# Mamba core of a hybrid backbone: decays requested ahead, token-major group sums, the first two output chunks together

## What is computed

```python
# 32 heads in 8 groups of 4; head width 64, state 128, chunk of 128 tokens
cb = jnp.einsum('bclgn,bcsgn->bgcls', cc, bc)
y_diag = jnp.einsum('bgcls,bgrcls,bcsgrp->bclgrp', cb, decay_in, x)
y_off = jnp.einsum('bclgn,bcgrpn,bgrcl->bclgrp', cc, prev_states, jnp.exp(a_cs))
y = y_diag + y_off                       # forward, and flipped for backward
y = y + d_skip * xs
y = y * jax.nn.silu(z)
yg = y.reshape(b, L, SSM_GROUPS, SSM_INNER // SSM_GROUPS)
yg = yg * lax.rsqrt(jnp.mean(yg * yg, axis=-1, keepdims=True) + EPS)
h = h + mod[:, :, 5] * ((yg.reshape(b, L, SSM_INNER) * norm_w) @ out_w)
```

## Time and profile before

| | us |
|---|---|
| median of 3 runs | 2073.91 |
| lowest, highest | 2071.22, 2076.09 |
| the profiled execution | 2077.36 |
| its span in the profile | 2075.5 |
| PE busy in the span | 1993.5 (96%) |
| DVE, ACT, POOL busy | 1295.8, 677.1, 203.0 |

### The profile page before, as it was taken

The page is one execution under the profiler, slowest core; times in us unless marked ns, Lnnn a source line. Parts: engine busy times, 40 slices in busy tenths (PEclk is TensorE's granted clock), DMA queues, the critical chain, the costliest instruction groups (busy, mean ns, idle before and its releaser), DMA issues. The chain is left out here.

```text
span 2075.5 us, 24931 instructions
## 1 busy us (share of the span) xinstructions
PE 1993.5 (96%) x10168; PEld 1666.4 (80%) x10168; DVE 1295.8 (62%) x1816; ACT 677.1 (33%) x900; POOL 203.0 (10%) x140
## 2 busy tenths in 40 slices
PE   7999999999999989999999999999999988789998
PEld 4788888878888878888887888888788984489998
DVE  5655547687877675554677555476765768745544
ACT  4422222232211242222223222222443546534432
POOL 1000001100034300000110000011000004430001
PEclk9999999999999999999999999999999999899999
DMA  9544426543520244442645444265443526554554
GB/s 358 198 146 133 161 69 203 165 151 125 176 86 1 81 164 141 160 145 90 195 147 170 149 131 154 74 206 157 152 142 92 164 87 190 156 162 151 186 156 138
DMA packets 279297, 306.73 MB, mean 148 GB/s; under 512 B 9457, under 2 KB 249745, under 8 KB 277393
## 3 DMA queue, kind: packets, MB, share of 16 engines
q1 hardware_dynamic: 275392, 293.83, 44.5%
q10 hardware_dynamic: 3792, 11.34, 1.4%
HBM read 298.70 MB, written 6.43 MB: 147 GB/s over the span
## 5 line engine op out<-in xcount | busy, mean ns | idle before, releaser
L1541 PE MATMUL banks<-xh,wh 128*128 128x512 f32 (+1 forms) x2120 | 775.5, 366 | 19.8 <-DVE xl L994 13.8
L1542 PE MATMUL banks<-xl,wh 128*128 128x512 f32 (+1 forms) x2120 | 771.6, 364 | 0.0
L1543 PE MATMUL banks<-xh,wl 128*128 128x512 f32 (+1 forms) x2120 | 771.4, 364 | 0.0
L929 DVE TENSOR_TENSOR wl<-raw,wh 128x2048 fp32r<-128x2048 f32 (+1 forms) x195 | 404.1, 2072 | 277.7 <-ACT wh L575 276.7
L575 ACT ACTIVATE wh<-raw 128x2048 fp32r<-128x2048 f32 (+1 forms) x201 | 349.8, 1740 | 637.4 <-PE banks L1543 557.8
L1541 PEld LDWEIGHTS banks<-xh,wh 128*128 128x128 f32 x2120 | 403.5, 190 | 88.4 <-issue 15.4
L1543 PEld LDWEIGHTS banks<-xh,wl 128*128 128x128 f32 x2120 | 403.3, 190 | 62.5
L1542 PEld LDWEIGHTS banks<-xl,wh 128*128 128x128 f32 x2120 | 403.8, 190 | 61.4
L1541 PE MATMUL banks<-gh,wh 128*128 128x512 f32 (+1 forms) x704 | 255.7, 363 | 3.7 <-DVE wl L929 2.5
L1542 PE MATMUL banks<-gl,wh 128*128 128x512 f32 (+1 forms) x704 | 255.2, 363 | 0.0
L1543 PE MATMUL banks<-gh,wl 128*128 128x512 f32 (+1 forms) x704 | 255.2, 362 | 0.0
(11 more groups left out here) (219 smaller groups left out, 1709.9 us busy)
## 6 DMA issues: line engine op xcount, KB each, us to landing
raw<-in_ffn_in SPq DMA_DIRECT2D x88, 1024.0 KB, 5.1
raw<-in_ffn_out SPq DMA_DIRECT2D x64, 704.0 KB, 4.8
ada_rawf<-in_ada_rest SPq DMA_DIRECT2D x60, 512.0 KB, 3.4
ada_rawo<-in_ada_rest SPq DMA_DIRECT2D x48, 512.0 KB, 3.3
raw<-in_mb_in_w SPq DMA_DIRECT2D x24, 1024.0 KB, 5.4
raw<-in_hy_in_w SPq DMA_DIRECT2D x12, 1024.0 KB, 5.2
afb<-decays SPq DMA_DIRECT2D x32, 256.0 KB, 4.7
raw<-in_mb_out_w SPq DMA_DIRECT2D x8, 1024.0 KB, 5.5
```

The lines of the kernel that those rows point to most:

```text
L929: dve.tensor_tensor(wl[n_slot][:, 0:cols], raw[r_slot][:, 0:cols], wh[n_slot][:, 0:cols].bitcast(F32), ALU.subtract).then_inc(w_lo, 1)
L1541: pe.matmul(dst, h, x_hi, start=start, stop=False)
L1542: pe.matmul(dst, h, x_lo, start=False, stop=False)
L1543: return pe.matmul(dst, l_, x_hi, start=False, stop=stop)
```

## The change

- **SP** runs one loop over 34 steps: at step h it requests afb of head h (after e_done and d_done count h-3, as before), then csx of head h-2 (after cs_used, as before). So csx stands two heads behind afb in the queue.
- **x of the latent tokens**: only x = 8 and 9 are turned and scaled ahead of b_dot_c(0). PE's turn_x(10 + 2g + p) stands behind the csx matmuls of pair p in groups 0 to 2 (bank 7), DVE's token_major(10 + 2g + r//2) behind exponents in heads 1 and 3 of these groups. d_x waits for the transposes it needs.
- **square_y** writes tt2 and tt3 in turn and waits for g_sum of two groups before.
- **Group sums** are token-major: for each 128-channel tile and token block the squares are the weights against a column of ones, so bank 0 holds 128x16. One root and one reciprocal work on 128x16 in `rs`; `spread(g)` is two transposes of a broadcast column. A root of `eps` stands ahead, behind head 31.
- **Output**: ACT copies chunk 0's high part to a new tile `mwh` ahead of square_y(8), and splits chunk 1 ahead of the ynh copies. DVE subtracts chunk 0 behind gate_y(8), chunk 1 behind the eight scalings, which have four buffers `ppn`. PE's `first_two(g)` takes five of the six matmuls of chunks 0 and 1 for each k-tile as ynl arrives; the sixth (wl of chunk 1) follows for all 16, then chunks 2 to 7. The loops over chunks are unrolled.

The diff:

```diff
@@ sync
-            for g in range(GROUPS):
-                for r in range(HPG):
-                    if g:
-                        sp.wait_ge(d_done, g * HPG + r - 3)
-                        sp.wait_ge(e_done, g * HPG + r - 3)
-                    sp.dma_start(afb[r][:], afscr[0, g * HPG + r].partition_broadcast(P)).then_inc(afb_in[r], 16)
-                    if g:
-                        sp.wait_ge(cs_used, 2 * g - 1 + r // 2)
-                    elif r == 0:
-                        sp.wait_ge(dt_v, 4)
-                    sp.dma_start(csx[r][:].rearrange("p (a n) -> p a n", a=2),
-                                 afscr[1, g * HPG + r].partition_broadcast(P)).then_inc(cs_in[r], 16)
+            sp.wait_ge(dt_v, 4)
+            for h in range(HEADS + 2):
+                if h < HEADS:
+                    if h >= HPG:
+                        sp.wait_ge(d_done, h - 3)
+                        sp.wait_ge(e_done, h - 3)
+                    sp.dma_start(afb[h % HPG][:], afscr[0, h].partition_broadcast(P)).then_inc(afb_in[h % HPG], 16)
+                c = h - 2
+                if c >= 0:
+                    if c >= HPG:
+                        sp.wait_ge(cs_used, c // 2 - 1)
+                    sp.dma_start(csx[c % HPG][:].rearrange("p (a n) -> p a n", a=2),
+                                 afscr[1, c].partition_broadcast(P)).then_inc(cs_in[c % HPG], 16)
@@ scalar
                 act.wait_ge(y_done, g)
-                if g > 1:
-                    act.wait_ge(g_sum, g - 1)
-                act.activation(tt[2][:], zsb[:, g * 2 - 2:g * 2, :].rearrange("p a n -> p (a n)"),
+                if g > 2:
+                    act.wait_ge(g_sum, g - 2)
+                act.activation(tt[2 + g % 2][:], zsb[:, g * 2 - 2:g * 2, :].rearrange("p a n -> p (a n)"),
                                ACT.Square).then_inc(g_sq, 1)
             def d_x(g):
+                act.wait_ge(tr_mm, 8 + 2 * (g // 2) + 2)
...
-            act.wait_ge(tr_mm, 16)
             d_x(0)
...
+            act.activation(rs[:, 24:25], eps[:], ACT.Sqrt)
+            act.wait_ge(raw_in[MBOUT.raw % 2], 16 * (MBOUT.raw // 2 + 1))
+            act.activation(mwh[:], raw[MBOUT.raw % 2][:], ACT.Copy).then_inc(w_hi, 1)
             square_y(GROUPS)
-            split_hi(MBOUT.w, CW, MBOUT.raw % 2, MBOUT.raw // 2 + 1, MBOUT.w)
             act.wait_ge(g_sum, GROUPS)
-            act.activation(tt[0][0:GROUPS, 0:L], bank[0][0:GROUPS, 0:L], ACT.Sqrt, bias=eps[0:GROUPS, 0:1],
+            act.activation(rs[:, 0:2 * GROUPS], bank[0][:, 0:2 * GROUPS], ACT.Sqrt, bias=eps[:, 0:1],
                            scale=1.0 / L).then_inc(g_rms, 1)
+            act.wait_ge(head_mm, HEADS)
+            r = MBOUT.raw + 1
+            split_hi(MBOUT.w + 1, CW, r % 2, r // 2 + 1, None)
...
+            r = MBOUT.raw + 2
+            split_hi(MBOUT.w + 2, CW, r % 2, r // 2 + 1, None)
+            for j in range(DT):
+                if 1 <= j < 6:
+                    chunk_hi(MBOUT, j + 2)
+                if j == 6:
+                    chunk_hi(ffn_in["11"], 0)
+                square(MBOUT, j // 2, j % 2, L)
@@ vector
+            for x in range(8):
+                token_major(x)
...
-            token_major(8, 2)
+            token_major(8)
+            token_major(9)
             b_dot_c(0)
             for h in range(HEADS):
                 products(h)
                 if h + 2 < HEADS:
                     exponents(h + 2)
                 g, r = h // HPG, h % HPG
+                if r % 2 and g < 3:
+                    token_major(10 + 2 * g + r // 2)
...
             gate_y(GROUPS)
+            dve.wait_ge(w_hi, MBOUT.w + 1)
+            r = MBOUT.raw % 2
+            dve.tensor_tensor(wl[MBOUT.w % 2][:], raw[r][:], mwh[:].bitcast(F32), ALU.subtract).then_inc(w_lo, 1)
             dve.wait_ge(g_rms, 1)
+            dve.reciprocal(rs[:, 0:2 * GROUPS], rs[:, 0:2 * GROUPS]).then_inc(g_rec, 1)
+            for g in range(GROUPS):
+                normed(g)
+            chunk_lo(MBOUT, 1)
+            for j in range(DT):
+                residual(MBOUT, 1, 5, j // 2, j % 2, L, MBOUT.w + j + 1)
+                if j < 6:
+                    dve.wait_ge(w_used, MBOUT.w + j + 1)
+                    chunk_lo(MBOUT, j + 2)
+                if j == 6:
+                    chunk_lo(ffn_in["11"], 0)
@@ tensor
-            for c4 in range(4):
-                turn_x(8, 0, c4)
-            pe.wait_ge(tr_out, 16)
+            turn_x(8)
+            turn_x(9)
...
                 pe.wait_ge(g_sq, g + 1)
                 for mt in range(2):
-                    ins = pe.matmul(bank[0][0:GROUPS, 0:L], sel[:, g, :], tt[2][:, mt * L:mt * L + L],
-                                    start=g == 0 and mt == 0, stop=g == GROUPS - 1 and mt == 1)
+                    for T in range(2):
+                        ins = pe.matmul(bank[0][:, 2 * g + T:2 * g + T + 1],
+                                        tt[2 + (g + 1) % 2][:, mt * L + T * P:mt * L + T * P + P], ones[:, 0:1],
+                                        start=g + mt + T == 0, stop=g == GROUPS - 1 and mt + T == 2)
                 ins.then_inc(g_sum, 1)
...
                     pe.wait_ge(cs_done, g * HPG + 2 * p + 2)
+                    pe.wait_ge(tr_out, 10 + 2 * (g // 2))
...
                     ins.then_inc(cs_used, 1)
+                    if g < 3:
+                        turn_x(10 + 2 * g + p)
...
+            def first_two(g):
+                for k in (2 * g, 2 * g + 1):
+                    h_, l_ = mwh[:, k * P:k * P + P], wl[MBOUT.w % 2][:, k * P:k * P + P]
+                    pe.matmul(bank[4][:, 0:L], h_, ynh[:, k, :], start=k == 0, stop=False)
+                    pe.matmul(bank[4][:, 0:L], h_, ynl[:, k, :], start=False, stop=False)
+                    ins = pe.matmul(bank[4][:, 0:L], l_, ynh[:, k, :], start=False, stop=k == IT - 1)
+                    h_ = wh[(MBOUT.w + 1) % 2][:, k * P:k * P + P]
+                    pe.matmul(bank[5][:, 0:L], h_, ynh[:, k, :], start=k == 0, stop=False)
+                    pe.matmul(bank[5][:, 0:L], h_, ynl[:, k, :], start=False, stop=False)
+                return ins
...
+            for g in range(5):
+                spread(g)
+            pe.wait_ge(w_lo, MBOUT.w + 1)
+            pe.wait_ge(w_hi, MBOUT.w + 2)
+            pe.wait_ge(h_done, MBOUT.h)
             for g in range(GROUPS):
+                if g + 5 < GROUPS:
+                    spread(g + 5)
+                pe.wait_ge(p_lo, MBN.q + g + 1)
+                ins = first_two(g)
+            ins.then_inc(w_used, 1)
+            pe.wait_ge(w_lo, MBOUT.w + 2)
+            for k in range(IT):
+                ins = pe.matmul(bank[5][:, 0:L], wl[(MBOUT.w + 1) % 2][:, k * P:k * P + P], ynh[:, k, :], start=False,
+                                stop=k == IT - 1)
+            ins.then_inc(w_used, 1)
```

146 lines of the change are left out of this document (68 added, 78 removed).

## The result

**2057.45 us** median (2054.41 to 2062.95) against 2073.75 for the kernel before in the same session: a ratio of 0.9925, with an interval of 0.9913 to 0.9937, or 16.3 us less. Timed once more beside another set of runs of before, the changed kernel gave 0.9935 (0.9920 to 0.9950). Forecast were 2056.8 us and -17.1 us.

The account below looks back on a forecast made before the run. PE, busy 96% of the span, was taken to bound most of the program, but not the stretch 1700 to 1860 us. Terms -8.9 + 2.4 - 1.8 - 8.8 = -17.1 on 2073.91 gave 2056.8 us, range 2049.5 to 2066.5.

Parts of the forecast that it names:

- Start of the core: Up to the first product: four scalings ahead instead of sixteen, first product at 1708.0 instead of 1716.85, -8.9 us.
- Groups 0 to 6: Seven core groups up to head 28: 70.5 us instead of 68.1, +2.4, bounds -0.4 to +6.8.
- ring through SP: Core groups: csx queued behind afb, which waits for exponentials; a group takes at least 5.1 + landing, 9.1 us at 4.0.
- Last group: From first product of head 28 to PE's end: 8.2 us instead of 10.0, -1.8 (0 to -2.5).
- The end: From PE's last head through chunk 7: first ynl at 5.3, chunk 2 at 21.7, end at 56.6; -8.8 us (-11.1 to -3).
- Last FFN: What follows chunk 7: costed at nothing, its first weights still requested after chunk 7's subtraction.
- 1 (the queue gives the core back): Rival, core: landings at 4.7 or above, groups 3 to 6 at 10.4; -11.2, 2062.7 us; chance 0.25.
- 2 (PE slow at the end): Rival, output projection: PE still falls to 1.2 GHz, first_two runs behind POOL; +5 taken, 2061.8 us; chance 0.10.
- 3: Rival, better than summed: DVE sets 8.6 a group (-2.8), POOL isn't held at the end (-2.3); 2051.7 us; chance 0.18.
- The signs named: Expected marks over core and end, such as 9.3 a group, and three marks of being wrong, one a group over 10.
- PE shows 0.50 from 1787 to 1805: Sign of being wrong, behind the last head: PE's granted clock at 0.50 in that stretch.
- If something outside 1700 to 1860 moves by more than 1 us: Sign of being wrong: any part outside the core and output projection stretch shifting by more than 1 us.

Follow-up runs that it names:

- b_scalings: Changed kernel with all sixteen scalings and eight latent turns ahead of b_dot_c(0) again; ratio 0.9951 to the kernel before.
- l_same: The changed kernel without an edit, timed again with a second profile; ratio 0.9935 to the kernel before.
- f_swap: Changed kernel with SP asking for csx of head h-2 ahead of afb of head h; ratio 0.9926 to the kernel before.
- a_queue: Changed kernel with SP asking for afb and csx of the same head together again, waits as before; ratio 0.9923 to the kernel before.
- c_square: Changed kernel with one buffer for the squares again, so ACT waits for the previous group's sums; ratio 0.9981 to the kernel before.
- the early request: Changed kernel requesting the last FFN's first weights one chunk earlier, after chunk 6's subtraction: ratio 0.9900; with csx also asked for ahead of afb: 0.9913.
- e_sums: Changed kernel with channel-major group sums again, root and reciprocal on 8x256, spread by one matmul a group; ratio 0.9962 to the kernel before.
- g_lolast: Changed kernel with DVE subtracting chunk 1's weights only after POOL has written all eight ynl; ratio 0.9937 to the kernel before.
- h_noread: Changed kernel with POOL writing zeros over csx instead of multiplying by C; ratio 0.9888 to the kernel before, 8.7 us faster than the changed kernel.

## Why the prediction was right, and where it was off

The median came 0.8 us from the forecast on the gain, and the forecast stands on the terms below; not all of its nearness is merit.

**Start of the core**: -8.9 forecast, -8.9 measured; undoing it moved the first product by 8.4, and the way there from the first scaling took the 12.95 us of before again. The core did start 1.7 us later than forecast, by what lay ahead of it: the last scalings begin at 1704.3 to 1706.1 in the thirteen profiles from the change on and at 1703.90 in the one of before. b_scalings, with the old order there, has 1705.08, so it isn't shown that the change is the cause.

**Groups 0 to 6**: +2.4 forecast. The mean of six profiles, 71.4, gives +3.3, the profile of the result +4.5, the second one +0.1. Groups 3 to 6 were forecast at 9.3 each and average 9.35; groups 0 to 2 at 33.3 together, and average 34.0. The size is right, but the step behind it is not, and that it came out so near is in part luck. The prediction had a ring through SP set 9.1 a group by the landing of csx, "with DVE at 8.6 close behind". It is the other way round: over the six profiles DVE is busy 9.1 of the 9.35 us of groups 3 to 6 (34.2 to 37.8 us of four groups that took 36.4 to 38.9). The holds had been counted at the 1.2 us a group of before, and were 11.6 us in the profile of the result for sixty differences (32.0 less 60 at 0.34), 1.5 a group. What the ring leaves in the rows are DVE's waits for b_dot_c, 3.3 us in three waits over the whole core of that profile and 1.1 in l_same, and moving csx earlier or later in the queue (f_swap, a_queue) changed nothing that can be timed. The ring bites where a hold of ACT is put into it (c_square).

The shortest landing in the changed kernel was 3.1 us, the median 3.8 for afb. The 2.6 that the prediction worked out from the Trainium skill was not reached; the section it names (DMA: Bandwidth & Descriptors, Anatomy of one DMA) gives its fit for DMAs that GpSimd issues, and these are issued by SP.

**Last group**: -1.8 forecast, -1.1 and -0.9 measured. This term was mis-sized: the 8.2 from first product to PE's end measured 7.9 to 10.6 in the same six profiles, mean 9.25.

**The end**: the first ynl forecast at 5.3 came at 6.1 and 5.9. Two steps were missing. The load of chunk 0's weights is requested behind the last csx and lands 8.0 us later, so ACT's copy of them begins at 1790.42 after a wait of 0.51 and pushes the squares and DVE's subtraction; and the spreads run at half clock. DVE's subtraction then ends 3.6 behind PE's end instead of 3.05, and the reciprocal, which stands behind it, starts then. The row of ynl (one gap of 2.0 for the 2.3 forecast) and chunk 2 at 22.2 and 22.0 (21.7) followed. -8.3 and -8.6 for -8.8.

**Last FFN**: costed at nothing, -2.1 and -1.5. Eleven profiles from the change on have 212.6 to 213.8 there (two more 208.7, with the early request), the one profile of before has 215.2. Nothing in it was changed. The rows place it in the second half of the FFN: behind 1990 us PE waited for DVE's split weights three times in the one profile of before, 2.5 us in all, and at the same distance from the end once, for 0.4, in the changed kernel's; from chunk 7's end to the first matmul of the FFN the two agree (8.10 and 8.05). That reads as an accident of the one profile of before, not as a gain of the change, but no second profile of before is there to show it.

**Rivals**: 1 (the queue gives the core back) is not what happened: afb landed in 3.8 at the median, not 4.7, and groups 3 to 6 stayed near 9.35. 2 (PE slow at the end) was rightly not the forecast, but for a reason that failed: the clock fell all the same, in spite of the shorter idle time, and in twelve of thirteen profiles it cost little, since PE stood waiting for ynl. The price taken for it, 5 us, is what e_sums shows (63.9 instead of 57.0 up to the end of chunk 7, less 1.6 for its later first ynl), with its longer spreads in it. 3 needed 8.6 in groups 3 to 6; DVE did set the pace, at 9.1, since the holds did not stay at 1.2, and a POOL that isn't held at the end (g_lolast) came without a measured gain.

**The signs named.** No group from 3 to 6 took over 10 in the changed kernel's two profiles (8.3 to 9.9). "PE shows 0.50 from 1787 to 1805" was met for 3.5 us, in the spreads. "If something outside 1700 to 1860 moves by more than 1 us" was met: the last FFN by -2.1 and -1.5. By its own signs, then, the prediction had two flaws that its total doesn't show.

## What to carry to other kernels

Undo each part of a change alone, and pairs of parts that share a queue: here requests ahead show no worth alone and need the second buffer. Before pricing a ring of waits, look at how busy the engines in it are over one turn: an engine with 96% leaves the ring nothing to set, and its held operations are the term to price. A load that stands last in an in-order queue holds not its consumer alone but all that the consumer's engine has queued behind it; follow that engine's next three instructions before costing it at zero. Price a stretch whose work is held at random from several profiles, since two of the same kernel differed by 4.4 us in it.

## What was not expected of the hardware

- TensorE's clock fell at the same place, behind the last head, in every kernel from the change on and stayed low there for 3.2 to 17.0 us, and no row found here tells how long it will be. Up to 7 us of it cost nothing that shows; e_sums' 17.0 cost about 5 together with its longer spreads.
- Two executions of one kernel differed by 4.4 us in seven groups, and 3.2 of that is how long POOL held DVE's differences (29.3 against 26.1 us).
- A faster core makes a hidden load visible. In h_noread ACT waited 2.79 us for chunk 0's weights, requested behind the last csx, and the first ynl came at 7.3 behind PE's end instead of 5.3 to 6.4:

```profile
1781.38 1.91 ACT L908 ACTIVATE mwh<-raw 128x2048 fp32r<-128x2048 f32 x1 [2.79 <-DMA raw<-in_mb_out_w]
```

- Over 512 columns POOL's memset took 0.52 us and its multiplication 1.27.
